# An adaLN modulation computed beside two MLPs: product and row sum moved from GpSimd and ScalarE to VectorE

## The reference, cut to what matters

```python
mod = jax.nn.silu(c) @ w_mod[l] + b_mod[l]
mod_c = jax.nn.silu(c_ctx) @ w_mod[l] + b_mod[l]
sh1, sc1, g1, sh2, sc2, g2 = jnp.split(mod[:, None, :], 6, axis=-1)
h = x * (1 + sc2) + sh2
x = _layer_norm(DEEPNORM_ALPHA * x + g2 * _sq_relu_mlp(h, w_fc1[l], w_fc2[l]), ln2_g[l], ln2_b[l])
```

## Time and profile before

| | us |
|---|---|
| median of 3 runs | 3192.93 |
| lowest, highest run | 3178.64, 3200.53 |
| the profiled execution, its own time | 3193.84 |
| its span, first to last instruction | 3192.5 |

### The profile page before, as it was taken

One profiled execution on the slowest core, in us unless ns is written; L12 is line 12 of the kernel. 1 busy time (PEld: TensorE's weight loads), 2 busy tenths in 40 slices (PEclk: granted clock), 3 DMA queues, 4 the chain that ended last, 5 costly groups with the idle time before them and its releaser, 6 DMA issues.

```text
span 3192.5 us, 39699 instructions
## 1 busy us (share of the span) xinstructions
PE 2938.5 (92%) x15940; PEld 2298.8 (72%) x15940; DVE 1619.0 (51%) x2154; ACT 1260.9 (39%) x2150; POOL 792.1 (25%) x528
## 2 busy tenths in 40 slices
PE   7989999898999879899999998998798999899998
PEld 4766667787878756676677776776566777678886
DVE  2655544636455546565444445637645565344433
ACT  4245443444444443454423335213543444442222
POOL 1022212665656631222201001000314333210000
PEclk8999999999999989999999999999999999899999
DMA  6222001455555512000232232211024454213222
GB/s 261 76 80 87 14 21 34 162 195 165 183 170 194 167 62 66 14 15 28 73 104 92 96 97 65 96 60 60 14 93 145 165 171 158 80 63 97 93 93 79
DMA packets 89198, 318.35 MB, mean 100 GB/s; under 512 B 10071, under 2 KB 12375, under 8 KB 88760
## 3 DMA queue, kind: packets, MB, share of 16 engines
q1 hardware_dynamic: 59040, 213.94, 20.4%
q10 hardware_dynamic: 29976, 101.88, 9.5%
HBM read 313.68 MB, written 2.10 MB: 99 GB/s over the span
## 4 chain that ended last, share of the span: by engine, by line
PE 49%; DVE 6%; ACT 5%; issue 2%; POOL 1%; DMA 0%; ACTq 0%; DVEq 0%; POOLq 0%
PE bank L675 24%; PE bank L679 12%; DVE t L1027 2%; PE bank L1111 2%; PE bank L2844 1%; PE bank L1128 1%; PE bank L1172 1%; PE bank L1572 1%; ACT t L490 1%; ACT t L926 1%; PE bank L1688 1%; ACT t L559 1%; PE bank L1950 1%; PE bank L2936 1%; PE bank L744 1%
## 5 line engine op out<-in xcount | busy, mean ns | idle before, releaser
L675 PE MATMUL bank<-t 128*128 128x512 f32 (+1 forms) x6432 | 1765.0, 376 | 91.3 <-ACT t L1005 31.9
L675 PEld LDWEIGHTS bank<-t 128*128 128x128 f32 x6432 | 1126.3, 192 | 350.5 <-issue 90.3
L679 PE MATMUL bank<-t 128*128 128x512 f32 (+1 forms) x3216 | 1074.1, 373 | 9.5 <-POOL t L935 5.5
L500 DVE TENSOR_TENSOR t<-t 128x1024 fp32r<-128x1024 f32 x350 | 493.2, 1412 | 478.2 <-ACT t L490 477.3
L679 PEld LDWEIGHTS bank<-t 128*128 128x128 f32 x3216 | 562.1, 191 | 128.8 <-POOL t L935 10.6
L597 POOL TENSOR_TENSOR t<-t 128x1024 f32<-128x1024 f32 x176 | 459.1, 2615 | 389.5 <-DMA t<-in_mod 388.5
L490 ACT ACTIVATE t<-t 128x1024 fp32r<-128x1024 f32 x350 | 366.1, 1049 | 367.0 <-PE bank L679 308.1
L692 DVE SCALAR_TENSOR_TENSOR t<-bank,t 128x512 f32<-128x512 f32 x192 | 129.3, 691 | 320.4 <-PE bank L679 304.9
L1312 POOL TENSOR_SCALAR t<-t 128x768 f32<-128x768 f32 (+3 forms) x160 | 126.3, 792 | 556.0 <-DVE t L1280 556.0
L1027 DVE TENSOR_TENSOR t<-t 128x512 f32<-128x512 f32 (+1 forms) x128 | 181.3, 1417 | 154.1 <-ACT t L1003 153.9
L559 ACT ACTIVATE t<-t 128x1024 f32<-128x1024 f32 x176 | 184.9, 1051 | 175.5 <-POOL t L597 175.5
(11 more groups left out here) (300 smaller groups left out, 2421.8 us busy)
## 6 DMA issues: line engine op xcount, KB each, us to landing
t<-in_mod ACTq DMA_DIRECT2D x176, 512.0 KB, 4.0
t<-in_l0fc SPq DMA_DIRECT2D x64, 512.0 KB, 3.8
t<-in_l1fc SPq DMA_DIRECT2D x64, 512.0 KB, 3.3
t<-in_s0fc SPq DMA_DIRECT2D x64, 512.0 KB, 3.6
t<-in_s1fc SPq DMA_DIRECT2D x64, 512.0 KB, 3.3
t<-in_mod SPq DMA_DIRECT2D x48, 512.0 KB, 4.5
t<-in_mixin SPq DMA_DIRECT2D x24, 512.0 KB, 3.3
t<-in_l0in SPq DMA_DIRECT2D x12, 512.0 KB, 3.5
```

The costliest lines, as they stand in the source:

```text
L500: dve.tensor_tensor(wlo[:, a % NR, :], raw[:, a % NR, :], whi[:, a % NS, :].bitcast(F32), ALU.subtract).then_inc(*up("dve_wlo", a))
L675: pe.matmul(acc.ap[:, o:o + m], w[:, ws], Hh[:, k, o:o + m], start=k == 0 and w is hi, stop=False)
L679: ins = pe.matmul(acc.ap[:, o:o + m], hi[:, ws], Hl[:, k, o:o + m], start=False, stop=k == NK - 1)
```

## The change

VectorE does a job alone: one instruction multiplies the weight tile by the condition and gives the row sum. ScalarE only sends the tiles; for each it waits until VectorE has done the job three places before. All four conditions are put through silu in the prologue, as columns; for a condition TensorE multiplies its columns, each repeated 128 times, by the identity into the two halves of a PSUM bank pair (b6 and b7), one step before it is due, and ScalarE copies both halves to `sil`. GpSimd only adds the bias when a layer's last job is done. The first job no longer waits for `h_end`. Left out below: `silu` is now made in place, the four condition columns are put into `vec`, and the input `conds` is gone.

```diff
--- before.py
+++ after.py
...
@@ -35,7 +35,7 @@
         at[name] = n
         n += k
-    for name in ("c", "c_ctx"):
+    for name in ("c", "c_ctx", "c_2", "c_ctx_2"):
         put(name, 8)
     for l in range(2):
         put(f"b_mod{l}", 48)
...
@@ -519,7 +518,7 @@
         DVEQ.wait_ge(*at("pool_cond", 0))
         DVEQ.wait_ge(*at("dve_own", "silu"))
-        dve.tensor_copy(cond[:, :, 0:2], silu.rearrange("p (v k) -> p k v", v=2)).then_inc(*up("dve_cond", 0))
+        dve.tensor_copy(cond[:, :, 0:4], sg.rearrange("p (v k) -> p k v", v=4)).then_inc(*up("dve_cond", 0))
     def mod_at(L, part):
         return at("pool_mod", L) if L else b6.after(("turn", L, part))
...
@@ -533,89 +532,84 @@
     def jobs_of(L, condition, s):
-        return [(L, condition, s, None, None)] + [(L, condition, s, part, m) for part in range(2 if s else 6) for m in range(NK)]
-    def modulation(name, sil, jobs, h_end, first, last):
-        def source(i):
-            L, condition, s, part, m = jobs[i]
-            return din["conds"][condition] if part is None else din[f"mod{L}"][NK * part + m]
-        def act_send(i):
-            act.dma_start(modw[:, i % NM, :], source(i)).then_inc(*up(f"job_in{i % NM}", (name, i), 16))
-        def act_job(i):
-            L, condition, s, part, m = jobs[i]
-            x = modw[:, i % NM, :]
-            if part is None:
-                ACTQ.wait_ge(*at(f"job_in{i % NM}", (name, i)))
-                if i:
-                    ACTQ.wait_ge(*at("pool_product", (name, i - 1)))
-                act.activation(sil[:, :], x, ACT.Exp, scale=-1.0).then_inc(*up("act_job", (name, i)))
-            else:
-                ACTQ.wait_ge(*at("pool_product", (name, i)))
-                act.activation(x, x, ACT.Copy, accum_out=modt[L][:, NK * part + m, s:s + 1]).then_inc(*up("act_job", (name, i)))
-            if i and i - 1 + NM < len(jobs):
-                ACTQ.wait_ge(*at("act_job", (name, i - 1)))
-                ACTQ.wait_ge(*at("pool_product", (name, i - 1)))
-                act_send(i - 1 + NM)
+        return [(L, condition, s, None)] + [(L, condition, s, j) for j in range(16 if s else 48)]
+    def modulation(name, sil, jobs, first, last):
+        tiles_ = [i for i, job in enumerate(jobs) if job[3] is not None]
+        number = {i: n for n, i in enumerate(tiles_)}
+        def due(step):
+            return range(*(len(jobs) * max(0, min(x - first, last - first)) // (last - first) for x in (step, step + 1)))
+        def act_send(n):
+            L, condition, s, j = jobs[tiles_[n]]
+            act.dma_start(modw[:, n % NM, :], din[f"mod{L}"][j]).then_inc(*up(f"job_in{n % NM}", (name, n), 16))
+        def pe_step(step):
+            for i in due(step + 1):
+                L, condition, s, j = jobs[i]
+                if j is None:
+                    for h, bank in enumerate((b6, b7)):
+                        PEQ.wait_ge(*bank.claim((name, "condition", i)))
+                        for k in range(4):
+                            ins = pe.matmul(bank.ap[:, P * k:P * k + P], spread(cond[:, 4 * h + k, condition:condition + 1]),
+                                            mat("ident"), start=True, stop=True)
+                    ins.then_inc(*up("pe_condition", (name, i)))
         def act_step(step):
             if step == 0:
                 ACTQ.wait_ge(*at("pe_mod", seq.mods[seq.mod_keys[-1]]))
-                for i in range(NM):
-                    act_send(i)
-            if step == first:
-                ACTQ.wait_ge(*h_end)
+                for n in range(NM):
+                    act_send(n)
             for i in due(step):
-                act_job(i)
-        def due(step):
-            return range(*(len(jobs) * max(0, min(x - first, last - first)) // (last - first) for x in (step, step + 1)))
+                if i in number:
+                    n = number[i]
+                    if n + NM < len(tiles_):
+                        ACTQ.wait_ge(*at("dve_job", (name, n)))
+                        act_send(n + NM)
+                else:
+                    ACTQ.wait_ge(*at("pe_condition", (name, i)))
+                    if i:
+                        ACTQ.wait_ge(*at("dve_job", (name, number[i - 1])))
+                    for h, bank in enumerate((b6, b7)):
+                        act.activation(sil[:, 512 * h:512 * h + 512], bank.ap,
+                                       ACT.Copy).then_inc(*bank.freed((name, "condition", i), "act"))
         def dve_step(step):
             for i in due(step):
-                if jobs[i][3] is None:
-                    DVEQ.wait_ge(*at("act_job", (name, i)))
-                    dve.tensor_scalar(sil[:, :], sil[:, :], 1.0, 1.0, ALU.add, ALU.mult).then_inc(*up("dve_own"))
-                    DVEQ.wait_ge(*now("dve_own"))
-                    dve.reciprocal(sil[:, :], sil[:, :]).then_inc(*up("dve_job", (name, i)))
+                L, condition, s, j = jobs[i]
+                if i in number:
+                    n = number[i]
+                    x = modw[:, n % NM, :]
+                    DVEQ.wait_ge(*at(f"job_in{n % NM}", (name, n)))
+                    dve.scalar_tensor_tensor(x, x, 1.0, sil[:, :], ALU.mult, ALU.mult,
+                                             accum_out=modt[L][:, j, s:s + 1]).then_inc(*up("dve_job", (name, n)))
+                else:
+                    DVEQ.wait_ge(*b6.after((name, "condition", i)))
+                    DVEQ.wait_ge(*b7.after((name, "condition", i)))
         def pool_all():
-            for i, (L, condition, s, part, m) in enumerate(jobs):
-                x = modw[:, i % NM, :]
-                if part is None:
-                    POOLQ.wait_ge(*at("dve_job", (name, i)))
-                    pool.tensor_tensor(sil[:, :], x, sil[:, :], ALU.mult).then_inc(*up("pool_product", (name, i)))
-                    POOLQ.wait_ge(*at("pool_product", (name, i)))
-                else:
-                    POOLQ.wait_ge(*at(f"job_in{i % NM}", (name, i)))
-                    pool.tensor_tensor(x, x, sil[:, :], ALU.mult).then_inc(*up("pool_product", (name, i)))
-                if i == len(jobs) - 1 or i >= 3 and jobs[i - 2][0] != jobs[i - 3][0]:
-                    pool_bias(L if i == len(jobs) - 1 else jobs[i - 3][0], i if i == len(jobs) - 1 else i - 3)
-        def pool_bias(L, i):
-            POOLQ.wait_ge(*at("act_job", (name, i)))
-            for s in range(1 if L == 3 else 2):
-                n = 16 if s else 48
-                x = modt[L][:, 0:n, s]
-                pool.tensor_tensor(x, x, v(("b_mod", "ada_b")[L // 2] + str(L % 2), 0, n), ALU.add).then_inc(*up("pool_own"))
-                POOLQ.wait_ge(*now("pool_own"))
-            for part, s in ((1, 1), (1, 0), (4, 0))[1 if L == 3 else 0:]:
-                x = modt[L][:, NK * part:NK * part + NK, s]
-                pool.tensor_scalar(x, x, 1.0, 1.0, ALU.add, ALU.mult).then_inc(*up("pool_own" if part == 1 else "pool_mod",
-                                                                                  L if part == 4 else None))
-        return act_step, dve_step, pool_all
-    cs, sg = vec[:, 0:16], small[:, 0:16]
+            for i, (L, condition, s, j) in enumerate(jobs):
+                if i == len(jobs) - 1 or jobs[i + 1][0] != L:
+                    POOLQ.wait_ge(*at("dve_job", (name, number[i])))
+                    for s in range(1 if L == 3 else 2):
+                        n = 16 if s else 48
+                        x = modt[L][:, 0:n, s]
+                        pool.tensor_tensor(x, x, v(("b_mod", "ada_b")[L // 2] + str(L % 2), 0, n), ALU.add).then_inc(*up("pool_own"))
+                    POOLQ.wait_ge(*now("pool_own"))
+                    for part, s in ((1, 1), (1, 0), (4, 0))[1 if L == 3 else 0:]:
+                        x = modt[L][:, NK * part:NK * part + NK, s]
+                        ins = pool.tensor_scalar(x, x, 1.0, 1.0, ALU.add, ALU.mult)
+                        ins.then_inc(*(up("pool_mod", L) if part == 4 else up("pool_own")))
+        return pe_step, act_step, dve_step, pool_all
+    cs, sg = vec[:, 0:32], small[:, 0:32]
     def act_prologue():
         act.dma_start(vec[:, :], din["vec"]).then_inc(*up("vec_in", 0, 16))
...
@@ -959,12 +953,11 @@
             r2 = [sb(s, [P, n]) for _ in range(2)]
             N = Norm(after, ranges, [sb(s, [P, n]) for _ in range(4)], centered, updated_at(keys, after, centered), weights)
             pe_by, act_by, dve_by = beside(s) if beside else [lambda t: None] * 3
-            act_step = dve_step = pool_all = None
+            pe_step = act_step = dve_step = pool_all = None
             if jobs:
-                h_end = at("pool_x" if L < 2 else "pool_hlo", (htag, NK - 1))
-                act_step, dve_step, pool_all = modulation(name, sb(s, [P, 1024]), jobs, h_end, 2, 62)
+                pe_step, act_step, dve_step, pool_all = modulation(name, sb(s, [P, 1024]), jobs, 2, 62)
             begin_stage("pool")
```

(12 more changed lines are left out.)

3 lines of the change are left out of this document (1 added, 2 removed).

## The result

The changed kernel takes 3100.3 us (median of 4 runs, 3098.7 to 3101.7), the kernel before 3187.9 us beside it (4 runs, 3178.6 to 3200.5). The ratio is 0.9722, with a 95% interval of 0.9685 to 0.976: faster by 2.8%. The forecast was 3128 with a range of 3104 to 3165. The direction was right; the gain was larger than any that the range allowed, and case C (3111, TensorE's floor) was the nearest. So the lower end was missed by no more than scatter, the forecast of 3128 by far more. The profiled execution has a span of 3097.4 us, 95.1 less than the one before.

A forecast was written before the change was run, and what follows sets the result against it. TensorE was taken to bound the kernel, by its standing still and its lower clock. 93.4 us recoverable less 10.5 for spreads, 12.5 and 5 for remaining stalls gave 65.4 us: 3193.8 to 3128 us, range 3104 to 3165.

The forecast's parts named there:

- case C: Both MLPs: changes to fc2 no longer stall and only TensorE's floor is left; 82.9 us gained, 3111 us; chance 0.13.
- Where the time lay: Stages l0 and s0, which carry the modulation: 70.8 and 22.6 us to be had, 93.4 us in all.
- the shared start of a stage: l0's first tiles and clock coming up: not all recoverable, so 8.5 us were taken off its 79.3 us loss.
- I keep half of what the four changes cost now.: Changes from fc1 to fc2: half the present stalls stay, 12.5 of 25.0 us in l0 and 5 of 9.9 in s0.
- The loop: An fc1 step through the engines' queues against TensorE's tile: 8.5 us against 8.32 in l0, 5.72 against 5.71 in s0.
- The job: VectorE's product with row sum over 1024 columns: 1.285 us plus 0.165 for the sum's read, 1.45 us.
- The spread: TensorE's spreading of a condition, unhidden between tiles: 2.09 us each, 10.5 us for five, 8.4 in l0 and 2.1 in s0.
- Who held TensorE up: Ring of waits among GpSimd, ScalarE and VectorE; GpSimd's product stretches VectorE's square L1027 to 3089 ns in l0, 2870 in s0.
- Rival B: VectorE's product with row sum runs at half rate, 2.52 us a job, in the fc1 halves: slower, 3208 us; chance 0.07.
- Rival A: Tile transfers take GpSimd's place, VectorE and ScalarE waiting for landings: 1 us a step gives 3154 us; chance 0.23.
- The range: Whole kernel: 3104 us (C with spreads at 7 us, a little less at the start) to 3165 (A's better half).

The follow-up runs named there:

- e3: Kernel before with conditions spread by TensorE, tiles sent right behind ScalarE's own sum and no late start; product stays on GpSimd, sum on ScalarE: 3126.2 us, ratio 0.98.
- e6: As e3 (product on GpSimd, sum on ScalarE, conditions spread by TensorE), but with sends one job late as in the kernel before: 3145.9 us, ratio 0.9875 to the kernel before.
- e13: As e6, with VectorE again taking each condition's reciprocal, in four pieces of 256 columns, before GpSimd may use it: 3184.0 us, ratio 0.9987 to the kernel before.
- e5: Kernel before with one change: ScalarE sends the tile three places on right behind its own row sum, one job earlier: 3169.0 us, ratio 0.9934.
- e7: Changed kernel with one more VectorE pass over each job's tile (maximum of the tile and itself): 3199.4 us, ratio 1.0043 to the kernel before.
- e4: Changed kernel with GpSimd running two idle passes of one source each beside every job: 3161.2 us, ratio 0.9904 to the kernel before.

## Why the prediction was right or wrong, point by point

*Where the time lay.* Right in place: both stages, and nothing else moved for the change. The 22.6 us for s0 stood (21.1 and the one spread of 1.8). For l0 the first working gave 79.3 us and the prediction then took 8.5 off because "the shared start of a stage (first tiles, clock coming up) is not all recoverable". That was wrong: 70.0 us gained and 7.1 paid for spreads are 77.1. The start's loss lay ahead of 558.2, where the sum began, and so was not in it. Over the very stretch of that sum, from the third tile to the start of the last sums, the changed kernel has

```profile
554.44 0.94 PE L669 MATMUL bank<-t 128*128 128x512 f32 x4
...
1087.95 0.62 PE L730 MATMUL bank<-t 128*32 128x512 f32 x2 [1.11 <-ACT t L754]
```

533.5 us against 1159.8 - 558.2 = 601.6, or 68.1 less; the three spreads in it are 5.3, and 62 tiles that take 8.40 us and no longer 8.32 are 5.0. 68.1 + 5.3 + 5.0 = 78.4: the loss of 79.3 us was read rightly and came back in full. The comparison with s1, on which the 8.5 rested, was off too: a tile takes 5.60 us there (the additions at 2877.15 and 2882.75, say), not two thirds of 8.32.

*"I keep half of what the four changes cost now."* This is the term that failed most: 17.5 us, measured nothing. The loop was worked out at 8.5 us against 8.32, with a job of 1.45; by the measured pitch it is 5.3 + 2.2 x 1.15 = 7.8. That is under TensorE's tile, so no slip builds up at all. The slack that the same paragraph had counted would have covered even the 8.5; keeping half was caution and had no row behind it. No run shows the 12.5 and the 5 us: no wait for L1002 is left in either stage.

*The job.* 1.285 us without the sum was estimated, 1.218 with it measured, and the read of the sum costs nothing between jobs. The slope was drawn from instructions of 512 and 768 columns of two other lines, and did not hold: from 768 to 1024 columns 200 ns are added, not 267.

*The spread.* 2.09 us each, measured 1.78: 10.5 us against 8.9. The row it was taken from ran at the lower clock (granted 0.50), those of the changed kernel at 1.00.

By the terms, l0: 49.9 forecast, 70.0 measured; the difference of 20.1 is 12.5 (changes) + 8.5 (start) + 1.3 (spreads), less 2.2, which the slower tiles more than account for. s0: 15.5 and 21.1; 5.0 and 0.3, and 0.3 over. The 4.0 outside is scatter.

*Who held TensorE up.* Wrong in its weights, though no number of the sum hung on it. "The square of L1027 is what the GpSimd product spoils" is true of the kernel before, and it is one way in which the loss reached TensorE there (25.0 us of waits for L1005 in l0). But that a product falls on the square is not fixed: with the new conditions and prompt sends (e3) all products remain and only 18 us of l0's loss are left, and none of s0's. Two things that the prediction passed by had set the jobs' timing. The reciprocal, of which it said that its gain "is in the sums above", is worth 38 us beside the products (e6, e13), the lag of the sends 21 (e5, and e3 against e6), and what was left for the move to VectorE after them is 26 (e3 against the changed kernel). In another order the shares could be others: no run has the jobs on VectorE and the old conditions. A sum made from the total loss of a stage comes out whatever the cause, so that it came out says nothing of the cause.

*Rival B.* The job at half rate didn't happen. A product with row sum, both sources in SBUF and in float32, takes 1218 ns for 1024 columns where the plain difference L500 takes 1226 in the earlier trace rows. The Trainium skill's sentence (Vector Engine (DVE) Microarchitecture Reference, "Points that are easy to get wrong"), that this family "halves throughput" with two such sources, isn't borne out here.

*Rival A* had a chance of 0.23; 1.4 us of waits say no. That they came from "not slow landings" was right: landings became no quicker (median 4.3 us against 3.8) and the waits went. That "most of those waits came from late sends" is not shown: sends one job earlier took only 39 of 183 us of them away (e5).

*The range.* Its lower end was case C with a little less for the spreads. It stopped 4 us short of the first median, because C itself contained the 8.5 us that were taken off.

## What to carry to other kernels

When work beside a matmul stage is moved between engines, write the step's loop through all queues and compare it with TensorE's tile: below it nothing is lost, above it each step pays, and e7 shows that this holds to a few us. A loss measured as "stage minus its quiet twin" can be forecast as regained in full once that loop is clearly below the tile; taking a share off for safety needs a row. And before blaming the many instructions that look slow, look for a single long one in a queue that many short ones pass (here five reciprocals, with the handover to and from them), and for what sets the time at which the slow ones meet.

## What the runs showed of the hardware that had not been expected

A GpSimd pass with one SBUF source holds a VectorE instruction with two up as well: 1218 ns became 2054 (e4), and 3.40 us in one meeting with a product of two sources (e1). Which of VectorE's instructions the products meet goes with the length of a stage: s0 took 397.4 us where they met the square, and 376.4 (e3) and 387.9 (e5) where they met the low part. The read of VectorE's row sum takes 81 ns and is hidden between jobs (pitch 1.15 us); ScalarE's takes 185. In l0 TensorE went through a tile in 8.32 us in the kernel before and in 655.61 - 647.21 = 8.40 us in the changed one, at the same granted clock of 1.00; this is 5 us over 62 tiles. The jobs' place isn't the cause: e3 and e6, with the old jobs, have 8.40 too, and e5, the kernel before with other sends, 8.32. In s0 a tile takes 5.60 us in both kernels. The cause stays open.
